# Four spacers in the on-chip memory plan of a two-block fp32 transformer kernel

## The reference, cut to what matters

```
first block:   h = rmsnorm(x); proj = h @ w_in
               y = [mla(...), fox(...), chunk_rel(...)]      three kinds of attention, 4 heads each
               x = x + rmsnorm(y) @ w_o
               x = x + cross(rmsnorm(x), rmsnorm(mem)) @ w_co
               x = x + (silu(h @ w_gate) * (h @ w_up)) @ w_down
second block:  pool mixer: u, z = h @ a_w_in; four groups of 512 channels, each pooled over
               2, 4, 8 or 16 tokens, times a 512x512 matrix, gated by silu(z), @ a_w_out
               sliding-window attention, 16 heads, gated, @ b_w_out
output:        rmsnorm(x)
```

## Time and profile before

| | |
|---|---|
| median of 3 runs | 2430.15 us (2428.74 to 2436.74) |
| the profiled execution | 2434.64 us, of which the trace spans 2432.8 us |
| TensorE busy with matmuls | 2369.6 us, 97% of the span |
| TensorE busy with weight loads | 1967.0 us (beside the matmuls) |
| VectorE, ScalarE, GpSimd busy | 1508.2, 833.1 and 1272.2 us |

### The profile page before, as it was taken

The page is one execution under the profiler, slowest core; times in us unless marked ns, Lnnn a source line. Parts: engine busy times, 40 slices in busy tenths (PEclk is TensorE's granted clock), DMA queues, the critical chain, the costliest instruction groups (busy, mean ns, idle before and its releaser), DMA issues.

```text
span 2432.8 us, 32824 instructions
## 1 busy us (share of the span) xinstructions
PE 2369.6 (97%) x11802; PEld 1967.0 (81%) x11810; DVE 1508.2 (62%) x1909; ACT 833.1 (34%) x1588; POOL 1272.2 (52%) x724
## 2 busy tenths in 40 slices
PE   7999999999999999999999999999999999999998
PEld 6887788888877888888888878878788787888887
DVE  6725555634577787877787678763754766045555
ACT  4211545612433222222222433231232333055663
POOL 4433964144144666666668344673746633465523
PEclk9999999999999999999999999999999999999999
DMA  6511000021011333333331111111221113100023
GB/s 213 160 44 44 1 1 27 10 113 44 18 40 48 113 121 121 121 121 121 121 121 65 48 44 44 56 66 52 69 82 56 56 65 130 52 27 19 27 104 131
DMA packets 67270, 177.31 MB, mean 73 GB/s; under 512 B 6846, under 2 KB 13760, under 8 KB 65112
## 3 DMA queue, kind: packets, MB, share of 16 engines
q1 hardware_dynamic: 58344, 148.58, 17.9%
q10 hardware_dynamic: 8816, 27.25, 3.2%
HBM read 160.04 MB, written 15.72 MB: 72 GB/s over the span
## 4 chain that ended last, share of the span: by engine, by line
PE 84%; DVE 7%; issue 4%; POOL 3%; ACT 2%; DMA 0%; SPq 0%; DVEq 0%; POOLq 0%; ACTq 0%
PE ps L691 22%; PE ps L692 22%; PE ps L694 22%; PE ps L843 6%; PE ps L821 5%; PE ps L831 3%; POOL split_lo L1597 1%; DVE h_lo L565 1%; DVE trail L3218 1%; PE ps L704 1%; PE ps L706 1%; PE ps L705 1%; PE ps L487 1%; DVE h_lo L568 1%; ACT p L971 0%
## 5 line engine op out<-in xcount | busy, mean ns | idle before, releaser
L691 PE MATMUL ps<-h_hi,split_hi 128*128 128x512 f32 (+1 forms) x1576 | 629.6, 399 | 20.5 <-DVE h_lo L568 13.8
L692 PE MATMUL ps<-h_lo,split_hi 128*128 128x512 f32 (+1 forms) x1576 | 613.5, 389 | 0.0
L694 PE MATMUL ps<-h_hi,split_lo 128*128 128x512 f32 (+1 forms) x1576 | 548.3, 389 | 0.0
L1473 POOL TENSOR_TENSOR split_hi<-raw,cf 128x1024 fp32r<-128x1024 f32 x70 | 136.9, 1955 | 496.9 <-PE ps L694 389.5
L691 PEld LDWEIGHTS ps<-h_hi,split_hi 128*128 128x128 f32 x1576 | 298.4, 189 | 81.3 <-issue 12.8
L694 PEld LDWEIGHTS ps<-h_hi,split_lo 128*128 128x128 f32 x1576 | 297.6, 189 | 62.0
L692 PEld LDWEIGHTS ps<-h_lo,split_hi 128*128 128x128 f32 x1576 | 298.5, 189 | 56.0 <-issue 1.2
L1548 POOL TENSOR_TENSOR split_lo<-raw,split_hi 128x512 fp32r<-128x512 f32 x144 | 231.2, 1624 | 201.5 <-ACT split_hi L2486 201.3
L1597 POOL TENSOR_TENSOR split_lo<-raw,split_hi 128x512 fp32r<-128x512 f32 x96 | 147.6, 1546 | 171.9 <-ACT split_hi L2644 171.7
L1475 POOL TENSOR_TENSOR split_lo<-raw,split_hi 128x1024 fp32r<-128x1024 f32 x70 | 195.3, 2789 | 5.5
L2486 ACT CAST split_hi<-raw 128x512 fp32r<-128x512 f32 x144 | 86.6, 622 | 287.0 <-PE ps L694 212.9
(11 more groups left out here) (447 smaller groups left out, 5136.4 us busy)
## 6 DMA issues: line engine op xcount, KB each, us to landing
raw<-in_strips SPq DMA_DIRECT2D x208, 256.0 KB, 2.7
raw<-in_strips SPq DMA_DIRECT2D x86, 512.0 KB, 3.5
ada_raw<-in_ada SPq DMA_DIRECT2D x64, 512.0 KB, 3.9
memw_raw<-in_mem_strips SPq DMA_DIRECT2D x8, 512.0 KB, 6.5
xT<-in_xT ACTq DMA_DIRECT2D x4, 1024.0 KB, 7.9
x_spill_d<-xT ACTq DMA_DIRECT2D x1, 3584.0 KB, 9.9
xT<-x_spill_d ACTq DMA_DIRECT2D x2, 1792.0 KB, 10.3
out_T<-out_sb SPq DMA_DIRECT2D x14, 256.0 KB, 2.3
```

The lines of the kernel that those rows point to most:

```text
L691: pe.matmul(acc[:, a:b], w_hi, hi[:, a:b], start=first, stop=False)
L692: pe.matmul(acc[:, a:b], w_hi, lo[:, a:b], start=False, stop=False)
L694: mm = pe.matmul(acc[:, a:b], w_lo, hi[:, a:b], start=False, stop=last)
L1473: pool.tensor_tensor(hi, raw[:, r, :], ones[:, 0:1].to_broadcast([P, D]), ALU.mult).then_inc(hi_split, 1)
```

## The change

The plan gets four spacers: 256 bytes behind the weight tiles (`before_high`), 16 bytes (rounded up to 32) between the high and the low tiles of the activation (`between`, and the same again as `g1`, `g2` and in the length of `mla_qkv` in the layouts that share that space), and 32 bytes before `sum_hi` (`g3`). Everything that is allocated behind a spacer moves up. No instruction is added, removed or moved on any engine; the streams of the two programs differ in addresses alone.

```diff
         split_lo = sb("split_lo", [P, 2, 8, P], F32R)
+        sb("before_high", [P, 64])
...
-        mla_q, mla_k, mla_v, q_hi, q_lo = shared([
-            ("mla_q", [P, HEADS, T], F32), ("mla_k", [P, HEADS, T], F32), ("mla_v", [P, QT, HALF], F32),
+        mla_q, mla_k, _, mla_v, q_hi, q_lo = shared([
+            ("mla_q", [P, HEADS, T], F32), ("mla_k", [P, HEADS, T], F32), ("g1", [P, 4], F32), ("mla_v", [P, QT, HALF], F32),
...
-        chk_stack, chk_khi, chk_klo = shared([("chk_stack", [P, HEADS, T], F32R), ("chk_khi", [P, HEADS, T], F32R),
-                                              ("chk_klo", [P, HEADS, T], F32R)])
-        _, p1, pt1 = shared([("mla_qkv", [P, 3 * HEADS, T], F32), ("p1", [P, 4, HALF], F32), ("pt1", [P, 4, HALF], F32)])
-        h_hi, h_lo = sb("h_hi", [P, NK, T], F32R), sb("h_lo", [P, NK, T], F32R)
+        chk_stack, chk_khi, _, chk_klo = shared([("chk_stack", [P, HEADS, T], F32R), ("chk_khi", [P, HEADS, T], F32R),
+                                                 ("g2", [P, 4], F32), ("chk_klo", [P, HEADS, T], F32R)])
+        _, p1, pt1 = shared([("mla_qkv", [P, 3 * HEADS * T + 4], F32), ("p1", [P, 4, HALF], F32), ("pt1", [P, 4, HALF], F32)])
+        h_hi = sb("h_hi", [P, NK, T], F32R)
+        sb("between", [P, 4])
+        h_lo = sb("h_lo", [P, NK, T], F32R)
...
-        (act_hi, act_lo, rms3, form_sums, quad_tmp, ada_acc, gated, sum_hi, sum_lo, ada_raw, ada_part, sum_quarters) = shared([
+        (act_hi, act_lo, rms3, form_sums, quad_tmp, ada_acc, gated, _, sum_hi, sum_lo, ada_raw, ada_part, sum_quarters) = shared([
...
-            ("sum_hi", [P, 3, 4, HALF], F32R), ("sum_lo", [P, 3, 4, HALF], F32R),
+            ("g3", [P, 8], F32), ("sum_hi", [P, 3, 4, HALF], F32R), ("sum_lo", [P, 3, 4, HALF], F32R),
```

## The result

The changed kernel takes 2456.11 us, median of 4 runs (2452.99 to 2456.86), against 2431.24 us for the kernel before (4 runs, 2428.74 to 2436.74). The ratio is 1.0098, with a 95% interval of 1.0085 to 1.0111: slower by 25 us, where 80 us less was forecast and 2436 was the upper end. Lines have moved by 3: L694, L695 and L697 are now the three matmuls of `product`, L824 makes scores, L846 multiplies by values.

The account below looks back on a forecast made before the run. TensorE's 512-column matmul spacing was taken as the bound. Savings of 82.6 + 8.7 = 91.3 us, 0.9 on the path (82), less 2 for waits, gave 80 us: 2350 us against the 2430.15 median, range 2334 to 2436.

Parts of the forecast that it names:

- What bounds the kernel: Whole kernel: TensorE, busy 2369.6 of 2432.8 us, sets the end by how fast 512-column matmuls follow each other.
- The address counts, and 128 is worse than 0: `pool_sums` and `p_lo` matmuls: 233 ns at distance 128 against 226.7 at 0, at the upper clock alone.
- The masks: Attention's bf16 mask matmuls: next start 0.05 us later at distance 256, 0.06 at 0; mean durations 219 and 221 ns.
- the floor of 2.7 ns: 512-column matmuls at distances near 256: 2.7 ns left over the columns, 216.0 ns each.
- the 10.7 ns per matmul: Saving for each of 7720 matmuls leaving distance 0, from 226.7 to 216.0 ns.
- the 82.6 + 8.7 us: TensorE savings: 82.6 us from 7720 matmuls leaving distance 0, 8.7 us from 512 leaving distance 128.
- The 13.3 ns are a conflict that another distance avoids: 512-column matmuls: 13.3 ns over their columns come from two conflicting TensorE reads, which distances near 256 avoid.
- Rival A: `product` matmuls: only `h_hi`, at 256, gains, not tiles at the other three distances; faster, chance 0.18.
- Rival B: fp32r loads: the distance does nothing, only the 128 case is repaired, 3 us, 2427 us; chance 0.15.
- Rival C: Moving tiles: new distances are as bad as 128, 7720 matmuls at 233 ns, +44 us, 2474 us; chance 0.21.
- 0.9 of the excess: Critical path: 90% of the change in TensorE's matmul time reaches the kernel's time.

Follow-up runs that it names:

- pool0: Kernel before with its 128-byte spacers made 512 bytes, so `pool_sums` and `p_lo` reach distance 0: 2429.3 us against 2428.98, ratio 1.0001.
- map2: Separate program without the reference's computation: finer distances, the order of `product`, then bf16; fp32r blocks 230.0 to 239.8 ns a matmul at finer distances, bf16 215.8 to 216.1.
- only256: Kernel before with the change's first spacer alone, 256 bytes behind the weight tiles: 2431.13 us, ratio 1.0000.
- map1: The map of distances: separate program, TensorE alone working, blocks of 48 fp32r matmuls at 16 distances from the weights; 226.7 ns a matmul at 0, 233.4 at 32.
- map3: Separate program without the reference's computation, varying weight width, moving-piece length and high/low pairs: 13.3 to 20.8 ns over the columns for 512-column matmuls.
- all32: Kernel before with one 32-byte spacer behind the weights, all moving tiles at distance 32, `pool_sums` and `p_lo` at 160: 2468.78 us, ratio 1.0159.
- low32: The change without `before_high` and `g3`, leaving the 32 bytes between high and low tiles: 2457.59 us against 2428.98, ratio 1.0117.
- abs256: Kernel before with a 256-byte spacer ahead of the weight tiles, distances in `product` kept: 2430.4 us against 2430.31, ratio 1.0002.

## Why the prediction was wrong, point by point

- *What bounds the kernel:* held. TensorE's matmuls are the end, before and after, and about 34 us more of them made 25 us more time.
- *The address counts, and 128 is worse than 0*: held. The map has 233.4 at 128 and 226.7 at 0, and pool0 brings `pool_sums` from 233 to 227. That it counts at the upper clock alone held too: 426.7 ns at 288 after the change, as at 0.
- *The masks*: **this is the step that failed.** The 0.01 us and 2 ns between two groups of masks were read as the gain of distance 256. The prediction itself said that what follows the masks differs, and took them for comparable since the weight load beside them has the same form. The exchange showed that they keep their times when the distances are swapped. And nothing was to be had from them: they are bf16, and in bf16 map2's 512-column matmuls take the same 216 ns at each of four distances. With that the floor of 2.7 ns fell, and with it the 10.7 ns per matmul and the 82.6 + 8.7 us. In its place the runs have 226.5 ns at distance 256 (only256), the same as at 0, and 233.4, 229.1 and 234.1 ns at 288, 320 and 416 (map1), where the forecast had 216.0 for all four.
- *The 13.3 ns are a conflict that another distance avoids:* not borne out. Of 24 distances below 256 none beats 0, and in the best case of map3 with 512 columns, a narrower load at its own best distance (96 columns at 32), it is still 13.3.
- *Rival A*, with its 0.18, had `h_hi` alone gain, at 256, and not the tiles at the other three distances. That was the right question, and only256 answers it: 26 matmuls at 256 take 226.5 ns each, as at 0, and nothing gains. Behind 256 the cost goes up and down: map1 has 226.9 ns there, 233.3 at 288, 229.2 at 320 and 234.2 at 416.
- *Rival B* had for it that `h_hi` at 384 and at 0 both showed 0.24 us before fp32 weights; that those loads are of another type kept it from being evidence for the fp32r stream. That the distance does nothing in such a stream, map1 and map2 refute: the same stream takes 226.7 to 239.8 ns by its addresses alone with every other engine idle. That TensorE waits for another engine's accesses, no run here shows.
- *Rival C* was right in kind, and by the row that it rested on: 0 is a minimum, and the one other fp32r distance on show was worse. Why 0 is one stays open: that two reads march in step, as it supposed, no run shows. Its price was mis-sized twice, both times upwards. It let all 7720 matmuls pay 6.3 ns; they pay 4.4 on average (about 34 us over 7720), because 256 is 0 modulo 256 and 64 costs little, so that two of three matmuls on `h` pay only for their neighbour. all32, where really all pay, has about 47 us (46 to 48 by how the starts are counted) and +39.8, close to its 48.6 and 44. And it let 0.9 of the excess reach the time: it was about 0.7 after the change, 0.8 in low32 and 0.85 in all32, in part since waits on VectorE shrink when the matmuls slow down. In pool0 nothing of 3.4 us could be seen.
- *The chances:* C had 0.21 and was left out of the range. For a distance of 32 the trace had one row (128, worse than 0) that read the same type in the same place, and one (the masks) that read another type in another. The first should have weighed more.

## What to carry to other kernels

Put fp32r moving tiles at the same address modulo 256 as 128-column weight tiles, high and low alike, for pieces of 512 columns (226.7 ns a matmul in map1, 229.1 to 234.1 at the other multiples of 32), and don't put small gaps between them: 32 bytes cost 1 to 1.6% here (2456.11 us after the change, 2457.59 in low32, 2468.78 in all32). A natural experiment in a trace is only as good as what stands ahead of and behind the instruction in both places and as the match of types; where two groups differ in their neighbours, a difference of 2 ns can't be put down to the suspected cause until one kernel swaps it. And a change on the bounding engine has to be set against the waits beside it: between nothing and about 85% of what the matmuls lost or gained arrived.

## What the runs showed of the hardware that was not expected

- In a stream on one moving tile and weights of 128 columns, the mean spacing of fp32r matmuls of 512 columns goes by the distance between moving tile and weights modulo 256 bytes: 226.7 ns at 0, 229.1 at 64, 233 to 234 at the other multiples of 32, up to 239.8 at 20 bytes. 256 bytes added to the address of everything changes nothing (abs256).
- A matmul at distance 0 pays 5 ns when it stands between two at distance 32 (227, 236, 232, 233). A fixed pair of addresses has no fixed cost: at distance 128 the spacings are 229 and 238 ns in turn, and the pair at 0 and 256 took 1380 ns for one round and 1360 for those behind it.
- The best distance depends on the width of the weight load: 0 for 128 columns, 32 for 96, 160 for 64 (of the four tried), and a load of 32 columns costs as much on average as one of 128 (18.1 and 18.3 ns). It depends on the length of the moving piece too: 160 for 256 columns.
- fp32r matmuls of 128 columns with whole weight loads start 110.5 to 111.7 ns apart, twice their columns (map3).
- bf16 has none of it (215.8 to 216.1 ns at distances 0, 32, 64 and 128), and neither has fp32r at a granted clock of 0.50 (426.7 ns at 0 and at 288).
